# High part and rest side by side in the last feed-forward stage: one 512-column product for both, sums made at the drain

## The reference, cut to what matters

```python
xl = post_norm(xl, 0.5 * g3 * swiglu(modulate(xl, sh3, sc3), ffn2_w_in[l], ffn2_w_out[l]))
```

## Time and profile before

| | |
|---|---|
| median of 3 executions | 2087.27 us |
| profiled execution | 2088.37 us |
| its span, first to last instruction | 2086.6 us |
| busy TensorE / VectorE / ScalarE | 98% / 66% / 36% of the span |
| mean granted TensorE clock | 0.993 |
| stage m = 5 | about 1880 us to the end |

### The profile page before, as it was taken

How to read it: one execution, slowest core, us unless ns; L and a number is a source line. 1 busy time by engine, 2 the same in 40 slices (tenths; PEclk the granted TensorE clock), 3 DMA queues, 4 the chain that set the end, 5 groups by cost and what they waited for, 6 DMA issues and landing times. The chain is left out here.

```text
span 2086.6 us, 30241 instructions
## 1 busy us (share of the span) xinstructions
PE 2052.6 (98%) x12718; PEld 1784.8 (86%) x12718; DVE 1373.0 (66%) x2160; ACT 752.9 (36%) x934; POOL 150.7 (7%) x136
## 2 busy tenths in 40 slices
PE   9999999999999999999999999999999999999998
PEld 8979979888888988688888888988888899779998
DVE  5965975776775657557776775655555565666555
ACT  4464465221222544436221222521221242555333
POOL 0400500000002000020000002000000200010001
PEclk9999999999999999999999999999999999999999
DMA  6744654554543210322554543333442333124542
GB/s 239 242 146 141 243 171 159 187 198 162 200 170 123 98 40 6 107 81 108 189 198 162 201 170 123 122 139 109 176 151 90 123 153 141 41 65 154 189 171 90
DMA packets 69280, 301.39 MB, mean 144 GB/s; under 512 B 6176, under 2 KB 24224, under 8 KB 49184
## 3 DMA queue, kind: packets, MB, share of 16 engines
q1 hardware_dynamic: 66432, 290.06, 39.2%
q10 hardware_dynamic: 2720, 9.51, 1.2%
HBM read 298.50 MB, written 1.05 MB: 144 GB/s over the span
## 5 line engine op out<-in xcount | busy, mean ns | idle before, releaser
L446 PE MATMUL PS<-xh,wh 128*128 128x512 f32 (+1 forms) x3676 | 1008.8, 349 | 2.7 <-DVE OA L1827 0.9
L446 PEld LDWEIGHTS PS<-xh,wh 128*128 128x128 f32 x3676 | 663.4, 189 | 92.6 <-issue 1.5
L446 PE MATMUL PS<-xl,wh 128*128 128x512 f32 (+1 forms) x2086 | 710.6, 341 | 0.0
L358 ACT ACTIVATE wh<-raw 128x2048 fp32r<-128x2048 f32 (+4 forms) x221 | 377.3, 1708 | 314.2 <-PE PS L446 232.3
L362 DVE TENSOR_TENSOR wh<-raw,wh 128x2048 fp32r<-128x2048 f32 (+3 forms) x183 | 376.0, 2055 | 102.2 <-ACT wh L358 101.7
L446 PEld LDWEIGHTS PS<-xl,wh 128*128 128x128 f32 x2086 | 395.2, 189 | 44.1
L446 PE MATMUL PS<-HH,wh 128*128 128x512 f32 (+1 forms) x1276 | 349.8, 360 | 0.0
L1269 DVE CUSTOM_DVE_ANT_0 NRM<-SQ,CBR 128x1024 f32<-128x1024 f32 x240 | 283.9, 1220 | 5.8
L1193 ACT ACTIVATE SI<-PS 128x512 f32<-128x512 f32 (+1 forms) x88 | 47.9, 544 | 588.2 <-PE PS L446 572.8
L446 PEld LDWEIGHTS PS<-HH,wh 128*128 128x128 f32 x1276 | 228.7, 189 | 36.5 <-DVE wh L362 0.6
L446 PE MATMUL PS<-HL,wh 128*128 128x512 f32 (+1 forms) x638 | 229.5, 360 | 0.0
(11 more groups left out here) (409 smaller groups left out, 2386.2 us busy)
## 6 DMA issues: line engine op xcount, KB each, us to landing
raw<-ffi_dram SPq DMA_DIRECT2D x88, 1024.0 KB, 4.9
SQ<-adat_dram SPq DMA_DIRECT2D x120, 512.0 KB, 4.5
raw<-ffo_dram SPq DMA_DIRECT2D x64, 704.0 KB, 4.2
raw<-layer_dram SPq DMA_DIRECT2D x36, 1024.0 KB, 4.9
lent<-layer_dram SPq DMA_DIRECT2D x14, 1024.0 KB, 7.5
raw<-odd_dram SPq DMA_DIRECT2D x12, 1024.0 KB, 4.9
raw<-even_dram SPq DMA_DIRECT2D x9, 1024.0 KB, 4.8
raw<-eout_dram SPq DMA_DIRECT2D x4, 1024.0 KB, 4.8
```

Of the source, the lines that this page charges most:

```text
L358: act.activation(high(i)[:, 0:n], raw[:, i.slot, 0:n], ACT.Copy).then_inc(hi_done, 1)
L446: m = pe.matmul(out, w[rows, o:o + P], x, start=n == 0 and j == 0, stop=n == len(tiles) - 1 and j == 2)
```

## The change

In m = 5 the rest of x goes into columns 256 to 511 of `xh` and the rest of the hidden chunk into those of `HH`. `beside` issues two matmuls a tile: the high weights times all 512 columns, then the rest of the weights times the first 256. The bank then holds wh*xh + wl*xh on the left and wh*xl on the right, and the two are added at the drain.

```diff
+        def beside(pe, i, c, tiles, both, ready=None):
+            bank_ = 2 * i.par + c
+            for n, (o, k) in enumerate(tiles):
+                if ready is not None:
+                    pe.wait_ge(ready[0], ready[1] + n + 1)
+                m = pe.matmul(PS[:, bank_, :], high(i)[:, o:o + P], both[:, k, :], start=n == 0, stop=False, skip_group_check=True)
+                m = pe.matmul(PS[:, bank_, 0:T], low(i)[:, o:o + P], both[:, k, 0:T], start=False, stop=n == len(tiles) - 1, skip_group_check=True)
+            return m
...
-                dve.tensor_tensor(xl[:, k, 0:n], SQ[:, k, 0:n], xh[:, k, 0:n].bitcast(F32), ALU.subtract)\
+                dve.tensor_tensor(xh[:, k, T:2 * T] if m == 5 else xl[:, k, 0:n], SQ[:, k, 0:n], xh[:, k, 0:n].bitcast(F32), ALU.subtract)\
```

ScalarE (`gate`) and VectorE (`hidden`) at an input slab:

```diff
-                    act.activation(SI[:, i.par, 0:n], PS[:, 2 * i.par, 0:n], ACT.Silu).then_inc(on["gate_act"], 1)
+                    if m == 5:
+                        act.activation(two(HF[:, i.par, :]), PS[:, 2 * i.par:2 * i.par + 2, T:2 * T], ACT.Copy).then_inc(on["lows_in"], 1)
+                        act.wait_ge(drained[i.par], i.count(2, i.d // 2 + 1))
+                        act.activation(SI[:, i.par, 0:T], SI[:, i.par, 0:T], ACT.Silu).then_inc(on["gate_act"], 1)
...
+                    if m == 5:
+                        dve.wait_ge(on["lows_in"], half * FH + k + 1)
+                        dve.tensor_tensor(two(SI[:, i.par, :]), two(HF[:, i.par, :]), PS[:, 2 * i.par:2 * i.par + 2, 0:T], ALU.add)\
+                            .then_inc(drained[i.par], 1)
+                        dve.wait_ge(on["gate_act"], k + (h0 + 1))
+                        hf = SI[:, i.par, T:2 * T]
+                        ch.after(dve.tensor_tensor(hf, SI[:, i.par, 0:T], hf, ALU.mult))
```

VectorE at an output slab:

```diff
-                    add_residual(dve, m, l, j + 2, i, k, 2 * i.par, True)
+                    if m == 5:
+                        xk, g = X[:, k, 0:T], mod[:, l, j + 2, k, 0:1]
+                        ch.after(dve.scalar_tensor_tensor(out=xk, in0=PS[:, 2 * i.par, T:2 * T], scalar=g, in1=xk, op0=ALU.mult, op1=ALU.add))
+                        dve.scalar_tensor_tensor(out=xk, in0=PS[:, 2 * i.par, 0:T], scalar=g, in1=xk, op0=ALU.mult, op1=ALU.add)\
+                            .then_inc(drained[i.par], 1)
```

`ch.after` lets VectorE wait for the end of its own instruction. `pair_beside` takes the place of `dense_pair` in m = 5 with the same order of tiles: 512 and 256 columns for slab 0, 512 for slab 1, and slab 1's 256-column products at the end. The semaphore `ln_sixth`, on which `sum_late` for the seventh chunk of stage m = 4 waited, is gone: the two adds of the chunk before are followed by such a wait each instead:

```diff
-                if k == 7 and m == 4:
-                    dve.wait_ge(on["ln_sixth"], 1 + j)
                 mm = dve.tensor_tensor(NRM[:, j, 0:n], NRM[:, j, 0:n], (X, SQ)[j][:, k, 0:n], ALU.add)
-                mm.then_inc(on["ln_all" if k == 7 else "ln_sixth"], 1)
+                if k == 7:
+                    mm.then_inc(on["ln_all"], 1)
+                else:
+                    ch.after(mm)
```

More of the change, by code:

```diff
@@ L403, in dense_halved @@
                     wait_split(pe, i)
-                m = product(pe, PS[:, 2 * i.par + c, 0:n], i, [((c * KT + k) * P, xh[:, k, 0:n], xl[:, k, 0:n]) for k in range(KT)])
+                m = beside(pe, i, c, [((c * KT + k) * P, k) for k in range(KT)], xh)
             m.then_inc(slab_used, 1)
@@ L448, in product, with two @@
             return m
+        def two(ap):
+            return ap.rearrange("p (a t) -> p a t", a=2)
+        def beside(pe, i, c, tiles, both, ready=None):
[6 more added lines that the diff above has]
+            return m
@@ new lines, in dense_beside, with pair_beside @@
+        def dense_beside(pe, i, chunks, kts, both, ready=None):
+            slab_begin(pe, i)
+            for c in range(chunks):
+                m = beside(pe, i, c, [((c * kts + k) * P, k) for k in range(kts)], both, None if c else ready)
+            m.then_inc(slab_used, 1)
+        def pair_beside(pe, i, ready):
+            slab_begin(pe, i)
+            j = i + 1
+            for s, k in [(0, 0), (1, 0), (0, 1), (1, 1), (0, 2), (0, 3), (1, 2), (0, 4), (1, 3), (0, 5), (1, 4), (0, 6), (0, 7),
+                         (1, 5), (1, 6), (1, 7)]:
+                if (s, k) == (1, 0):
+                    pe.wait_ge(hi_done, HI[j.base] + 1)
+                    pe.wait_ge(drained[j.par], j.d // 2)
+                pe.wait_ge(on["xm_lo"], ready + k + 1)
+                for c in range(2):
+                    o = (c * KT + k) * P
+                    w = i + s
+                    mm = pe.matmul(PS[:, 2 * w.par + c, :], high(w)[:, o:o + P], xh[:, k, :], start=k == 0, stop=False, skip_group_check=True)
+                    if s == 0:
+                        mm = pe.matmul(PS[:, 2 * w.par + c, 0:T], low(w)[:, o:o + P], xh[:, k, 0:T], start=False, stop=k == KT - 1,
+                                       skip_group_check=True)
+                if (s, k) == (0, KT - 1):
+                    mm.then_inc(slab_used, 1)
+            wait_split(pe, j)
+            for k in range(KT):
+                for c in range(2):
+                    o = (c * KT + k) * P
+                    mm = pe.matmul(PS[:, 2 * j.par + c, 0:T], low(j)[:, o:o + P], xh[:, k, 0:T], start=False, stop=k == KT - 1, skip_group_check=True)
+            mm.then_inc(slab_used, 1)
@@ L469, in dense_pair @@
             slab_begin(pe, i)
[L470 to L487, removed]
+            for s in range(2):
+                if s:
+                    slab_begin(pe, i + s)
+                for k in range(KT):
+                    pair_terms(pe, i + s, k, n, (0, 1, 2), ready)
         def pair_in_halves(pe, m):
@@ L1137, in act_end_halves, with sum_late @@
             act_modulate_half(act, m + 1, 1)
-        def sum_late(dve, m, k):
+        def sum_late(dve, ch, m, k):
             n, (i, _) = WIDTH[m], last_slabs(m)[-1]
@@ L1163, in post_norm @@
             dve.wait_ge(on["ln_in"], SUMS_IN[m + 1])
-            sum_late(dve, m, 7)
+            sum_late(dve, ch, m, 7)
             statistics(dve, ch, u, slice(0, n // P))
@@ L1192, in gate @@
                     act.wait_ge(slab_used, i.count(4, i.base + 1))
-                    act.activation(SI[:, i.par, 0:n], PS[:, 2 * i.par, 0:n], ACT.Silu).then_inc(on["gate_act"], 1)
+                    if m == 5:
+                        act.activation(two(HF[:, i.par, :]), PS[:, 2 * i.par:2 * i.par + 2, T:2 * T], ACT.Copy).then_inc(on["lows_in"], 1)
+                        act.wait_ge(drained[i.par], i.count(2, i.d // 2 + 1))
+                        act.activation(SI[:, i.par, 0:T], SI[:, i.par, 0:T], ACT.Silu).then_inc(on["gate_act"], 1)
+                    else:
+                        act.activation(SI[:, i.par, 0:n], PS[:, 2 * i.par, 0:n], ACT.Silu).then_inc(on["gate_act"], 1)
                     if i.base in HALVED:
@@ L1225, in pe_ffn, with into @@
                 pair_in_halves(pe, m)
-            else:
-                dense_pair(pe, Idx(FIRSTS[m]), T, CHUNKS_AT[m])
+            elif m == 0:
+                dense_pair(pe, Idx(FIRSTS[0]), T, 0)
+            else:
+                pair_beside(pe, Idx(FIRSTS[m]), CHUNKS_AT[m])
+            def into(i, k):
+                if m == 5:
+                    dense_beside(pe, i, 2, KT, xh)
+                else:
+                    dense(pe, i, 2, KT, xh, xl, 0, n)
             for k in range(2, FH):
@@ L1231, in pe_ffn @@
                 else:
-                    dense(pe, Idx(FIRSTS[m] + k), 2, KT, xh, xl, 0, n)
+                    into(Idx(FIRSTS[m] + k), k)
             for half in range(2):
                 if half:
-                    runs_of(pe, f"ffi{f}{l}1", lambda i, k: dense(pe, i, 2, KT, xh, xl, 0, n))
+                    runs_of(pe, f"ffi{f}{l}1", into)
                 def down(i, k):
@@ L1239, in down @@
                         return
-                    dense(pe, i, 1, FH, HH, HL, 0, n, (on["h_lo"], hidden_before(m, half)) if k == 0 else None)
+                    ready = (on["h_lo"], hidden_before(m, half)) if k == 0 else None
+                    if m == 5:
+                        dense_beside(pe, i, 1, FH, HH, ready)
+                    else:
+                        dense(pe, i, 1, FH, HH, HL, 0, n, ready)
                 steps_of(f"ffo{f}{l}{half}", down)
```

21 lines of the change are left out of this document (13 added, 8 removed).

## The result

| | before | changed |
|---|---|---|
| median | 2087.86 us | 2096.55 us |
| lowest to highest of 7 executions | 2085.14 to 2091.68 | 2094.64 to 2098.86 |
| profiled execution, its span | 2088.37, 2086.6 us | 2098.86, 2097.1 us |

The changed kernel is slower: ratio 1.0049, 95% interval 1.0039 to 1.0058. I had 2095.0 us, +7.7; the medians differ by 8.7 us.

What follows compares the result with a forecast made beforehand. TensorE was taken to set the pace, with weight-slab preparation close behind; new stops and steps of some 14.7 us against 7.0 us from the products gave +7.7 us, 2095.0 us, range 2089.5 to 2099 us.

Steps and rivals of the forecast that it cites:

- The prices of the drain: Input slabs, from first drain S: copy 0.60 us, add 0.69, Silu 0.42; split_hi at S+1.69 instead of S+0.28, 1.41 us later.
- The stops: Input slabs: chain 5.97 us against 5.25 of room, so TensorE stops 0.72 us at every second slab.
- the second half's output slabs: ScalarE's Square waits for the two-step residual, split_hi queues behind it; every slab stops about 0.50 us, +2.3 us in this stretch.
- The tile: Last stage's products: a tile goes from 0.360 to 0.3467 us, 7.0 us less over 528 tiles.
- The stop at the second output slab: Turn from input to output products: VectorE does the last hidden chunk before the split; 1.26 us stop, once each half.
- The start: First slabs of the last stage: the longer drain delays the first following weight load by +1.2 us; Silu's table load fits under add.
- The norm ahead: Stage before: chunk 6's sums wait after each of two adds, delaying the next residual, +0.2 us.
- Rival 1: Input slabs: longer drain not in the next split's way; 2081.0 us, faster. Chance 0.07 in full, 0.11 in part.
- the break-even: Input slabs: at 0.69 us of added delay they stop no more, and the kernel takes 2087.3 us.
- Rival 2: Last stage's products: mixed widths save nothing, tile stays 0.360 us; 2099 us. Chance 0.10 together with rival 3.
- Rival 3: Drain: the two 512-wide reads take 0.7 and 0.8 us; 2097.5 us. Chance 0.10 together with rival 2.
- The granted clock: TensorE: stops lower its clock to 1.2 GHz, a slab at that level taking some 5 us more; chance 0.02.

Runs made afterwards that it cites:

- e5_order: Changed kernel with the split for slab i+2 put ahead of Silu in most input slabs, no instruction added or dropped: 2088.91 us, ratio 1.0014 to before.
- e1_products: Changed kernel's products with the drains of the kernel before, high weights times rest left out of the last stage's sums: 2084.3 us, ratio 0.9979 to before.
- e6_mixed: e5_order with first pair, each half's last input slab and second half's output slabs back to three 256-column products and one-step drain: 2084.47 us, ratio 0.9986 to before.
- e11_split_first: e7_mixed_grouped with the second half's output slabs merged too and their split put ahead of the Square: 2082.44 us, ratio 0.9979 to before.
- e7_mixed_grouped: e6_mixed with each chunk's 512-column products ahead of its 256-column ones: 2083.42 us, ratio 0.9991 to before.

## Why the prediction was right, point by point

**The direction and the mechanism** were right: TensorE's gain is more than spent by a drain that stands in ScalarE's queue ahead of the next split. e5_order shows it by moving the splits with no instruction added or dropped.

**The prices of the drain** held to 0.01 us: add at S+0.63, Silu at S+1.36, split_hi at S+1.68 (1.69 predicted). The stops come every second slab; two slabs take 11.92 us (1934.68 to 1946.60), 11.82 predicted. Once the start is over, a stop is 0.59 to 0.67 us and not 0.72, since slabs of 5.65 us leave the chain 0.1 us more room. In the second half's output slabs the stops are 0.47 to 0.53 us (0.50 predicted), at each half's second output slab 1.23 (1.26 predicted).

**The tile was the mis-sized term.** I took 0.3467 us by adding the two pure patterns, and kept 0.360 as the far bound; it is 0.353 in most slabs, so that the products save about 3.5 us (528 x 0.0067) and not 7.0. With 0.3533 in place of 0.3467 the same steps give 9.4 us in all, of which 9.2 lie in the stage; 9.32 was measured. So the tile explains 1.7 of the 1.8 us by which the traces miss the forecast.
The Trainium skill, page "TensorE: Matmul & The Clock Gate", section "Back-to-back issue gap", has 2.5 ns beside the columns of a warm product, a gap that it gives for a product by itself. By that the change would save 1.3 us. For one width the trace disagrees, with 13.3 ns; the saving of 3.5 us lies between my 7.0 and that 1.3.

**By stretch.** From the stage's start to the drain of slab 10 of the first half: +4.0 us (3.1 predicted). To the first drain of the second half: +0.5 (predicted 0.25, less a slab's gain). Its ten further input slabs: +2.0 (1.3, with an eleventh). From there to the square root: +2.9 (2.3 + 0.53). The excess sits where input slabs are, as the tile's 0.007 us ask, but for 0.2 us ahead of the first drain (below).

**The stop at the second output slab** came at the size that I gave; the wait for DVE's wh there is the longest of the 18, 1.2 us. But the cause that I named, VectorE doing the last hidden chunk ahead of the split, is only half of it. In the trace the hidden chunk ends at 1955.32 us and split_hi at 1955.34 (1953.97 + 1.37), so split_lo could not have started before 1955.37 without that chunk either: ScalarE's late split alone would give the same stop.

**The start.** Slab 1's drain lies 4.13 us behind slab 0's instead of 3.35, and slab 2's 6.59 behind that instead of 6.06: +1.3 us, 1.2 predicted. Silu's table load did not fit under the add, as I had it: it ran from 1893.60 for 1.28 us and ended 0.16 us after the add (1894.04+0.68). Before that, the first drain of the stage already came 0.20 us late: 12.00 us after the square root (1892.98 less 1880.98), where it was 11.80. I had nothing for that; the prediction says that where the low part is stored costs nothing. VectorE's first rest of the stage, before and changed:

```profile
1882.34 0.42 DVE L819 TENSOR_TENSOR xl<-SQ,xh 128x256 fp32r<-128x256 f32 x1
```
```profile
1883.93 0.43 DVE L855 TENSOR_TENSOR xh<-SQ,xh 128x256 fp32r<-128x256 f32 x1 [0.28 <-issue]
```

It starts 2.59 us after the square root before and 2.95 after the change, the delay put down to "issue". Every run here has these 2.95 us and the first drain at 12.0, also e1_products, which has the old drains, and e6_mixed, which also has three products of 256 columns for the pair. So the 0.20 us belong neither to the drain nor to the wide products, but to what all runs share, the storing side by side first of all; why they arise stays open.

**The norm ahead.** From the first sum to the next residual it was 0.73 us and is now 0.92 (1877.33 to 1878.25): +0.19, 0.2 predicted.

**The rivals.** Rival 1, the covered drain, is what e5_order and e11_split_first make true by another order: the drain's work could not fit in the 0.69 us of the break-even, but the split could be taken out from behind it. In e5_order it starts 0.49 us after S (1928.54 less 1928.05), under that bound, and the input slabs from slab 3 on have no stop. Rival 2, a tile of 0.360 us, came half true. Rival 3, dearer reads of two banks, did not: the copy takes 0.60 us and the add 0.69, as priced. The granted clock did not fall: it is 1.00 in each 10 us of the changed kernel from 1880 to 1990 us, with TensorE busy for as little as 8.49 us of ten.

```profile
1880.00:1890.00 10.00, 8.49 (x47) 6.82 (x46) 8.69 (x28) 8.50 (x15) 0.00 (x0) 1.00 0.12 48
```

## What to carry to other kernels

An engine that idles for 60% of a slab has no room for a longer drain if the step that the next slab waits for is queued behind that drain: before lengthening a drain, follow the queue from the moment the sums are ready to the next operand, and issue that operand's preparation first. With two buffers a chain that overruns its room by d stops every second slab here, so a pair of slabs loses d once and not twice. And do the costly drain only where something covers it, keeping the plain form at the start and at the turn from one kind of product to the next (e6_mixed, e7_mixed_grouped). In the last output slabs the costly one paid once the split went first (e11_split_first).

## What the runs showed of the hardware

A stream of products of one width keeps a fixed pace, 0.120 us for 256 columns and 0.2267 us for 512. A stream that alternates the two is not always their sum: tiles of 0.3467 and of 0.353 us, from the same instructions in one program, with either width first, and the difference lies in the wide product. Grouped by width within a chunk they take 0.349 us in both halves. On ScalarE and VectorE, by contrast, prices read from other instructions of the same engine, width and memory held to 0.01 us.
